# A recurrence on four quarters of the matmul array, with block-diagonal operands for two heads at once

## The reference, cut to what matters

```python
def step(state, inp):
    r_t, w_t, k_t, v_t, kk_t, a_t = inp
    sa = jnp.einsum('bhvk,bhk->bhv', state, -kk_t)
    state = (state * w_t[:, :, None, :]
             + sa[..., None] * (kk_t * a_t)[:, :, None, :]
             + v_t[..., None] * k_t[:, :, None, :])
    return state, jnp.einsum('bhvk,bhk->bhv', state, r_t)
_, y = lax.scan(step, s0, tuple(map(seq_first, (r, decay, k, v, kk, a))))
```

## Time and profile before

| what | value |
|---|---|
| median of 3 runs | 2769.58 us |
| the profiled execution's own time | 2771.98 us |
| its span (first to last record) | 2770.1 us |
| PE busy | 2617.0 us (94%), 28073 records |
| PEld busy | 2190.7 us (79%) |
| VectorE, ScalarE, GpSimd busy | 1563.2, 1318.0, 316.2 us |
| `rwkv` | from about 1210 to about 1762 us of the span |

### The profile page before, as it was taken

The page is one execution under the profiler, slowest core; times in us unless marked ns, Lnnn a source line. Parts: engine busy times, 40 slices in busy tenths (PEclk is TensorE's granted clock), DMA queues, the critical chain, the costliest instruction groups (busy, mean ns, idle before and its releaser), DMA issues. The chain is left out here.

```text
span 2770.1 us, 66149 instructions
## 1 busy us (share of the span) xinstructions
PE 2617.0 (94%) x28073; PEld 2190.7 (79%) x28073; DVE 1563.2 (56%) x2377; ACT 1318.0 (48%) x2272; POOL 316.2 (11%) x367
## 2 busy tenths in 40 slices
PE   6999999999999999989999999999999999999992
PEld 5989897777766766678999998888888888888882
DVE  4566664443035555544444444553326888888884
ACT  4645552222134444334444444552223777777771
POOL 0111222332000000001212121100001000000002
PEclk9999999999999999999999999999998999999996
DMA  4344332222132323313221201154345999999976
GB/s 111 148 167 145 125 138 89 92 93 74 37 96 65 99 68 102 114 38 81 55 69 52 64 21 33 48 152 129 121 185 219 397 395 395 395 396 395 395 301 258
DMA packets 162649, 440.53 MB, mean 159 GB/s; under 512 B 16295, under 2 KB 96825, under 8 KB 150097
## 3 DMA queue, kind: packets, MB, share of 16 engines
q1 hardware_dynamic: 146413, 381.95, 38.7%
q10 hardware_dynamic: 9060, 29.56, 2.8%
q0 software_dynamic: 6912, 25.17, 2.4%
HBM read 344.22 MB, written 92.41 MB: 158 GB/s over the span
## 5 line engine op out<-in xcount | busy, mean ns | idle before, releaser
L2671 DVE TENSOR_TENSOR ex_wL<-wx,ex_wH 128x2048 fp32r<-128x2048 f32 x192 | 436.1, 2286 | 46.5 <-ACT ex_wH L2575 43.8
L2575 ACT CAST ex_wH<-wx 128x2048 fp32r<-128x2048 f32 x192 | 366.4, 1912 | 96.3 <-PE ex_bank L2467 70.7
L2465 PE MATMUL ex_bank<-ex_wH,ex_xTH 128*128 128x512 f32 x512 | 199.4, 389 | 0.6 <-DVE ex_xTL L2676 0.6
L2467 PE MATMUL ex_bank<-ex_wL,ex_xTH 128*128 128x512 f32 x512 | 199.3, 389 | 0.0
L2466 PE MATMUL ex_bank<-ex_wH,ex_xTL 128*128 128x512 f32 x512 | 199.2, 389 | 0.0
L717 PE MATMUL ph_acc<-ph_wH,uH 128*104 128x512 f32 x480 | 191.5, 399 | 0.0
L717 PE MATMUL ph_acc<-ph_wH,uL 128*104 128x512 f32 x480 | 188.8, 393 | 0.0
L717 PE MATMUL ph_acc<-ph_wL,uH 128*104 128x512 f32 x480 | 188.6, 393 | 0.0
L419 PE MATMUL pf_acc<-uH,pf_wH 128*128 128x348 f32 x648 | 160.7, 356 | 6.4 <-DVE pf_wL L541 6.4
L419 PE MATMUL pf_acc<-uL,pf_wH 128*128 128x348 f32 x648 | 138.9, 323 | 0.0
L419 PE MATMUL pf_acc<-uH,pf_wL 128*128 128x348 f32 x648 | 138.3, 322 | 0.0
(11 more groups left out here) (416 smaller groups left out, 6879.5 us busy)
## 6 DMA issues: line engine op xcount, KB each, us to landing
wx<-in_expert_w_gate SPq DMA_DIRECT2D x32, 2048.0 KB
wx<-in_expert_w_up SPq DMA_DIRECT2D x32, 2048.0 KB
wx<-in_expert_w_down SPq DMA_DIRECT2D x32, 2048.0 KB
s_y<-ex_y ACTq DMA_DIRECT2D x32, 512.0 KB, 10.0
fw<-in_w_in SPq DMA_DIRECT2D x27, 512.0 KB
hw<-in_w_in SPq DMA_DIRECT2D x6, 2048.0 KB, 10.1
s_qkT<-ph_stg ACTq DMA_DIRECT2D x4, 2080.0 KB, 7.0
mb_gt<-s_pT SPq DMA_DIRECT2D x16, 512.0 KB, 3.6
```

The source lines that it names most:

```text
L2465: nc.tensor.matmul(out, aH, bH, start=first, stop=False)
L2467: return nc.tensor.matmul(out, aH, bL, start=False, stop=last)
L2575: nc.scalar.copy(wH[:, w, part], raw(j, s)[:, part]).then_inc(w_high, 1)
L2671: nc.vector.tensor_tensor(wL[:, w, part], raw(j, s)[:, part], wH[:, w, part], ALU.subtract).then_inc(w_low, 1)
```

## The change

- Inputs: one set of buffers instead of two. The next four heads' inputs are loaded in five pieces of 4 chunks (10 DMAs each), each piece when `seq` has passed its chunks. `x_in` becomes five semaphores.
- Place of a head: `across(e, h)` says on which half of the partitions the token-side data of head h of pair e lie: h for e = 0, 1 - h for e = 1. So products from channels to tokens (or back) of the four heads use all four quarters of the array: `masked`, the new `raw` (the old step 2), piece 1 of `seq`, the state update, the new `old_state`. The two pairs write different banks (0 and 1, or 6 and 7).
- Block-diagonal operands: `Md`, `Nd`, `Yd`, `Gd` hold the two heads' matrices on the diagonal of a 116 x 116 matrix whose rest is zero, so that one product over the full array serves both heads: steps 9, 11, 12, the masked products of `seq`, and piece 3. They are written in two instructions, one for each half of the partitions.
- `tokens`: GpSimd copies each input twice side by side (`two`, 3 copies a chunk), and six full-array transposes replace twelve small products. ScalarE takes the result out in two copies.
- Step 7 makes one product with 104 columns out of two (`X2` now has `Q0`'s matrix in its middle).
- `seq` has four pieces. The masked product with v of piece 1 is made one chunk ahead, in piece 2. R is made on VectorE, the old state's part of Y is a product of its own (`old_state`), copied by ScalarE (`Hs`) and added on VectorE. The new state and Y are in piece 4 together.
- A round has 8 pieces among its groups. Bank 7's role for `tokens` and the norm's transposes passes to banks 0 and 1, shared by `masked`, `raw`, `tokens`, `old_state` and the norm: each waits until the one before it has been read (`after_reading`).
- GpSimd clears `two`, `tok`, most of `Md`, `Nd`, `Yd` and `Gd` at the start of `rwkv` (8960 elements for each partition).
- In `project_recurrent` the norm's two parameter rows are loaded with 32 DMAs instead of 8, in the new order of heads; `load_branch` follows that order.

The diff, cut to its core:

```diff
+                    for e, h in ((0, 0), (0, 1), (1, 0), (1, 1)):
+                        at = NF * j + 2 * d + across(e, h)
+                        sp.dma_start(rows_[at:at + 1, RD * e:RD * e + RD], heads[e, h:h + 1]).then_inc(consts, 16)
...
+def across(e, h):
+    return h if e == 0 else 1 - h
...
-            return (first(2) + late(9) + tokens(A) + piece()
-                    + first(6) + late(10) + ahead(A + 2, 0) + piece()
-                    + first(7) + late(11) + ahead(A + 2, 1) + piece()
-                    + first(8) + late(12) + piece() + piece()
...
+            return (tokens(A) + copies(A + 2) + first(6) + late(10) + piece() + old_state(A - 2)
+                    + first(7) + raw(B) + late(11) + piece()
+                    + first(8) + late(12) + piece()
+                    + ahead(A + 2) + first(9) + piece()
+                    + tokens(B) + copies(B + 2) + second(6) + first(10) + piece() + old_state(B - 2)
+                    + second(7) + raw(A + 2) + first(11) + piece()
+                    + second(8) + first(12) + piece()
+                    + ahead(B + 2) + second(9) + piece())
...
+            def masked(ch):
...
+                for j in range(2):
+                    for e, h in PAIRS:
+                        last = mm(bank[row(e, h), e, 2 * j * TC:(2 * j + 2) * TC].rearrange("p (a t) -> p a t", a=2),
+                                  BK[half(h), e, j, cols], KR[half(h), e, :, cols], start=True, stop=True)
...
+            def raw(ch):
+                after_reading(n_read, ch + 1 + OPEN)
+                for e, h in PAIRS:
+                    last = mm(bank[row(e, h), e, 0:TC], KR[half(h), e, 0, cols], BK[half(h), e, 0, cols], start=True, stop=True)
...
-                    for e, h in PAIRS:
-                        last = mm(at(bq, 0, e, h), N8[here(h), ln, e, :], Q[here(h), ln, 0, e, :], start=True, stop=True)
+                    for e in range(2):
+                        last = mm(full(bq, e), both(Nd[0:PX, ln, e]), Q[0:PX, ln, 0, e, :], start=True, stop=True)
...
+            def tokens(ch):
+                after_reading(tok_read, ch + 1 + OPEN)
+                pe.wait_ge(twice, 3 * ch + 4 + OPEN)
+                for e in range(2):
+                    for j in range(3):
+                        last = tr(bank[0:PX, e, RD * (1 - e) + 2 * RD * j:RD * (1 - e) + 2 * RD * (j + 1)], two[:, ch % 3, e, j].rearrange("p n t -> p (n t)")[:, 0:PX], c.ident[:])
...
+            def seq(ch, q):
+                if q == 1:
...
+                        pe.wait_ge(y_done, ch + OPEN)
+                        pe.wait_ge(seq_dve, added(ch - 1))
+                        for e, h in PAIRS:
+                            last = mm(bank[row(e, h), 6 + e, 384:384 + RD], KR[half(h), e, 0, cols], S[half(h), t % 2, e, :], start=True, stop=True)
+                elif q == 2:
+                    pe.wait_ge(rest_done, ch + 1 + OPEN)
                     for e, h in PAIRS:
+                        last = mm(o(1, e)[here(across(e, h))], Qf[row(e, h), s, e, :], R[row(e, h), e, :], start=True, stop=True)
+                    if ch + 1 < NC:
+                        for e in range(2):
+                            last = mm(o(2, e), both(Md[0:PX, (ch + 1) % MS, e, 1]), tok[0:PX, (ch + 1) % TS4, 2, e, :], start=True, stop=True)
                 elif q == 3:
+                    for e in range(2):
+                        last = mm(o(0, e), both(Gd[0:PX, s, e]), RA[0:PX, 0, e, :], start=True, stop=True)
                 else:
+                    if t < NCH - 1:
+                        for j, right in ((0, lambda e, h: Uu[row(e, h), e, :]), (1, lambda e, h: tok[row(e, h), s, 2, e, :])):
+                            for e, h in PAIRS:
+                                mm(bank[half(h), 6 + e, 128:128 + RD], tok[row(e, h), s, j, e, :], right(e, h), start=(j == 0), stop=(j == 1))
                     for e in range(2):
+                        mm(o(2, e), both(Md[0:PX, m, e, 2]), tok[0:PX, s, 2, e, :], start=True, stop=False)
+                        last = mm(o(2, e), both(Md[0:PX, m, e, 0]), Uu[0:PX, e, :], start=False, stop=True)
...
+            def old_state(ch):
+                after_reading(h_read, carried(ch))
+                for e, h in PAIRS:
+                    last = mm(bank[row(e, h), e, 0:RD], KR[half(h), e, 1, cols], S[half(h), ch % NCH % 2, e, :], start=True, stop=True)
...
+            nc.gpsimd.memset(two[:], 0.0).then_inc(twice, 1)
+            nc.gpsimd.memset(tok[:], 0.0).then_inc(blank, 1)
+            nc.gpsimd.memset(Md[:, 2:MS], 0.0).then_inc(blank, 1)
+            nc.gpsimd.memset(Nd[:], 0.0)
+            nc.gpsimd.memset(Yd[:], 0.0).then_inc(blank, 1)
+            nc.gpsimd.memset(Gd[:], 0.0).then_inc(blank, 1)
```

More of the change, by code:

```diff
@@ L1306, in round_ @@
             A, B = 2 * r, 2 * r + 1
-            pieces = iter([(2 * r - 2 + j, q) for j in range(2) for q in (1, 2, 3, 4, 5)])
+            pieces = iter([(2 * r - 2 + j, q) for j in range(2) for q in (1, 2, 3, 4)])
             first = lambda n: [("solve", A, n)] if new else []
@@ L1323, in rwkv @@
-        SPREAD = {"sum0": 0, "sum1": 1, "mean": 2, "sub": 2, "sq": 3, "var0": 8, "var1": 9, "std": 11, "rin": 12, "nrm": 12,
-                  "t0": 17, "e0": 17, "t1": 18, "e1": 18, "t2": 24, "e2": 24, "add": 25, "gate": 25}
+            old_state = lambda ch: [("h", ch)] if old and ch % NCH > 0 else []
+            copies = lambda ch: [("two", ch)] if new and ch < NC else []
+            return (tokens(A) + copies(A + 2) + first(6) + late(10) + piece() + old_state(A - 2)
[6 more added lines that the diff above has]
+                    + ahead(B + 2) + second(9) + piece())
@@ L1465, in solve @@
-                last.then_inc(spe[ln], 1)
-            last_read = [(tok_emptied, 1 + OPEN)]
-            def tokens(ch):
-                d, z, cols = place(ch)
-                for x in last_read:
-                    pe.wait_ge(*x)
-                for j in range(3):
-                    for e, h in PAIRS:
-                        src = V[z][half(h), e, cols] if j == 2 else BK[z][half(h), e, j, cols]
-                        last = mm(bank[here(h), 7, (2 * j + e) * RD:(2 * j + e + 1) * RD], src, c.ident[half(h), half(h)], start=True, stop=True)
-                last.then_inc(tok_done, 1)
-                last_read[:] = [(tok_read, ch + 1 + OPEN)]
@@ L1548, in solve @@
                 four = bank[0:PX, bx, 0:4 * TC].rearrange("p (k e t) -> p k e t", k=2, e=2)
-                two = bank[0:PX, bx, 0:2 * TC].rearrange("p (e t) -> p e t", e=2)
-                what = {6: (X2[0:PX, ln], four), 7: (X4[0:PX, ln], four), 8: (N8[0:PX, ln], two),
-                        10: (Y1[0:PX, ln], two)}
+                two = bank[:, bx, 0:2 * TC].rearrange("p (e t) -> p e t", e=2)
+                what = {6: (X2[0:PX, ch % TS4, 0::2], four), 7: (X4[0:PX, ln], four)}
+                if n in (8, 10):
+                    act.wait_ge(*at_pe(ch, n))
+                    if ch < 2:
+                        act.wait_ge(blank, 4 + OPEN)
+                    for h in range(2):
+                        last = nc.scalar.copy((Nd if n == 8 else Yd)[here(h), ln, :, h, 0:TC], two[here(h)])
+                    last.then_inc(sact[ln], 1)
                 if n in what:
@@ L1653, in norm, with copies @@
                 ins.then_inc(gn["pool"], 1)
-            walk({"m": masked, "gn": norm})
+            def copies(ch):
+                d, cols = place(ch)
+                if d > 0 and ch % PIECE == 0:
+                    pool.wait_ge(x_in[ch % NCH // PIECE], 160 * d + OPEN)
+                if ch >= 3:
+                    pool.wait_ge(tok_done, ch - 2 + OPEN)
+                for e in range(2):
+                    nc.gpsimd.tensor_copy(two[:, ch % 3, e, 0:2, :, 0:TC], BK[:, e, :, cols].unsqueeze(2).to_broadcast([128, 2, 2, TC])).then_inc(twice, 1)
+                nc.gpsimd.tensor_copy(two[:, ch % 3, :, 2, :, 0:TC], V[:, :, cols].unsqueeze(2).to_broadcast([128, 2, 2, TC])).then_inc(twice, 1)
+            nc.gpsimd.memset(two[:], 0.0).then_inc(twice, 1)
[4 more added lines that the diff above has]
+            nc.gpsimd.memset(Gd[:], 0.0).then_inc(blank, 1)
+            pool.wait_ge(twice, 1 + OPEN)
+            walk({"two": copies, "m": masked, "gn": norm})
         @block.vector
```

347 lines of the change are left out of this document (185 added, 162 removed).

## The result

The changed kernel takes 3080.5 us (median of 3069.0 to 3116.2), the kernel before 2769.8: a ratio of 1.111, 95% interval 1.1086 to 1.1135. The forecast was 2922 us, the range 2790 to 2990. The direction was right; the time is 159 us above the forecast and outside the range.

What follows compares the result with a forecast made beforehand. PE was taken to bound `rwkv`, 95 to 96% busy at full clock. Chunks going from 6.76 to 8.6 us add 145 us, the start 8: 2771.98 becomes 2925, less 2.4 for the median, 2922 us; range 2790 to 2990.

Steps and rivals of the forecast that it cites:

- the period: Time from chunk to chunk in `rwkv`: 8.6 us instead of 6.76, from PE's work, norm transposes, waits and issue.
- Records of block-diagonal products, 0.10 us each: Weight load sets the pace of 28 full-array records a chunk: 2.80 us, where the same work took 1.50.
- (b): Rival: weight load of the block-diagonal records is hidden, 1.50 us a chunk instead of 2.80; 2820 us, chance 0.10.
- (c): Rival: full-array products cost only moving columns, tiling changes fall into gaps, copies and adds set the pace; 2717 us, chance 0.14.
- Changes of tiling, 0.145 us each, 10 a chunk: PE pays at each switch between quarter and full-array products: 1.45 us a chunk.
- Four quarters, twice as fast: `masked`, `raw`, piece 1, state update and `old_state` on all four quarters: 0.92 us a chunk instead of 1.83.
- rival (a): Third and fourth quarter bring nothing, no record starts sooner than 24 ns: 33 us more, 2955 us, chance 0.12.
- Waits 0.6 us, on `Hs` before `raw`: PE waits for ScalarE's copy to free the bank: 0.6 us a chunk in all, 0.1 of it before step 7.
- Start, 8 us: Once, at the start of `rwkv`: GpSimd's clearing and copies delay the first `tokens`, PE idles; 8 us, bounds 0 and 12.
- SyncE's added DMAs, 0: 24 more parameter-row DMAs of 0.29 us, ahead of the third tile's weights, nearly fit: 0 us, at most 3.
- Tokens 0.65: Six full-array token transposes in `tokens`: 0.65 us a chunk, against 0.69 before.
- VectorE and ScalarE still waiting for PE: Sign in `rwkv`: VectorE rising to 4.6 us a chunk and ScalarE to 4.4, both below PE's.

Runs made afterwards that it cites:

- run 1: Changed kernel with steps 9, 11 and 12 as two-quarter products out of the same block-diagonal buffers; 2899.7 us.
- run 14: Changed kernel with all block-diagonal products as two-quarter ones in the first 20 of 80 chunks, unchanged from chunk 20 on; 3011.0 us.
- run 6: Changed kernel with the products of steps 6, 8 and 10 issued twice, 24 more two-quarter products a chunk; 3108.7 us.
- run 11: run 8 with its 12 added full-array products a chunk moving 4 columns each in place of 52; 3371.9 us.
- run 9: Changed kernel with one pair of neighbouring products in `seq` swapped, 8 changes of tiling a chunk in place of 10; 3062.7 us.
- run 10: run 9 with step 9 also issued ahead of the masked products, 6 changes of tiling a chunk, all products kept; 3016.6 us.
- run 2: run 1 with the state's and the output's products as two-quarter products too; 2843.3 us.
- run 7: run 4 with 12 more full-array products of 52 columns a chunk, all ahead of step 9, results unread; 2904.3 us.
- run 8: run 7 with the same 12 added products in six pairs at six places, 12 changes of tiling where run 7 has 2; 3074.8 us.
- run 3: run 2 with the token transposes as twelve four-quarter products, one ScalarE copy instead of two, no GpSimd copies; 2807.8 us.
- run 4: run 3 with compact buffers in place of block-diagonal ones, fewer mask and copy instructions, no clearing of the buffers; 2773.2 us.
- run 13: run 8 with the 12 added full-array products only from chunk 20 of 80 on; 2915.5 us.
- run 12: run 4 with the next layer pair's inputs loaded in two pieces of 10 chunks in place of five of 4; 2782.7 us.

## Why the prediction was wrong

**The step that failed is the period.** "Period: 7.75 + 0.09 + 0.6 + 0.15 = 8.6 us" took every duration from rows at the full clock and multiplied by 79 as if the clock were given. The forecast names no clock at all. The changed stage holds the lower level for 41% of its time, and that is 128 of the 161 us by which the profiled execution missed (3086.2 against 2925). That the block-diagonal products bring it there is shown: with three steps of them undone the clock is back (run 1), and switched on from chunk 20 they bring it down again (run 14). Runs 6 and 11 show one thing that matters: with 48 fewer streamed columns a product the low level holds longer, and with more streamed products less of it is left. PE is 94 to 96% busy in all of these, so the busy share, on which the forecast leaned, can't tell.

What sets off each single fall is not shown. In the changed kernel and in runs 1, 6, 9, 10 and 14, every fall inside the stage comes within 4 us behind a wait for `Hs` of at least 0.5 us, or in one. The wait alone isn't enough (run 1, 73 waits and 2 falls; run 2, 92 and 1), and run 11 fell without. So few streamed (moving) columns beside many weight loads, and a wait on top, is the account that fits all the runs; it is argued and not shown. No run here takes the wait for `Hs` out of the changed kernel; that is the rival left untested.

Point by point:

- *Records of block-diagonal products, 0.10 us each*: right. 0.103 in run 7, 0.11 in the changed kernel. (b) and (c) are refuted.
- *Changes of tiling, 0.145 us each, 10 a chunk*: the count is right, the price too high. 0.08 us by runs 7 and 8, about 0.10 by L1473.
- *Four quarters, twice as fast*: right for 104 columns (0.022 us a record against 0.045). For the 52 columns of `raw` it is 0.022 against 0.024, nearly what rival (a) said. For 64 columns four records take 0.097 us in `old_state` and 0.082 on the mean in the state update, against 0.115. The Trainium skill, "TensorE: Matmul & The Clock Gate", section "Wait — 56ns, not 53.3ns?", has about 25 ns as the least distance from start to start. Taken singly, starts in different quarters lie 7 ns apart here, so the trace disagrees; taken over whole bursts, the four quarters need 20 to 24 ns a record.
- *Waits 0.6 us, on `Hs` before `raw`*: the place is right, 0.4 us measured there.
- *The sum at the full clock, 8.6*: 8.96 measured, within the 7.5 to 9.5 that was given; 29 us over the stage. The trace says where, if each record is given the time to the next one's start (us a chunk, the 32 chunks at 1.00, changes of tiling at 0.145 in the forecast):

```
                                        forecast                measured
four quarters, 3 changes behind them    0.92 + 0.44 = 1.36      1.69
two quarters, 2 changes                 1.93 + 0.29 = 2.22      2.41
block-diagonal, 4 changes               2.80 + 0.58 = 3.38      3.41
tokens, 1 change                        0.65 + 0.15 = 0.80      0.76
norm transposes                         0.09                    0.10
waits and issue                         0.60 + 0.15 = 0.75      0.59
```

  The largest mis-sized term is the four quarters: the new piece 1 and `old_state`, forecast at 0.115 us each, take 0.29 and 0.30 to the next start. Behind piece 1 the next weight load often waits for ScalarE's token copy while PE still counts as busy (PEld for `rw_tok`, 46 times in the stage, 10.4 us in all); the rest of the cause is open.
- *Start, 8 us*: 10, but 5.6 in the stage itself. *SyncE's added DMAs, 0*: what they cost is lost in the 4.5 us that arose before the stage, within the 6 us by which that point varies.
- *Tokens 0.65*: L1498 to L1448 is 0.75, a change included.
- *"VectorE and ScalarE still waiting for PE"*: right in the changed kernel, but their doubled instructions would have been the next bound: 35 us (runs 3 to 4), the start's share included.
- *What was not foreseen at all*: the range, 2790 to 2990, allowed each price to be wrong but not the rate at which all of them are paid.

The Trainium skill, "TensorE: Matmul & The Clock Gate", section "HAM oscillation — how this bites in real kernels", ties a clock that falls again and again to idle gaps between bursts of products. PE's waits here are short: the longest in the changed stage is 2.2 us and most are 0.5 to 0.7, and in run 11 it is busy 260.00 of 260.00 us at 0.50. So idle gaps of that size aren't what holds the clock down; that the falls come behind short waits fits a part for them. The measurement decides against reading that rule as the only cause.

## What to carry to other kernels

Before merging small products into wide ones, count the columns that each weight load serves, and the places where the tiling changes: 52 columns behind 116 weight columns cost 0.10 us where two small ones side by side cost 0.05, and each place 0.08 more. Where a change puts weight loads and changes of tiling in place of streamed columns, forecast it at both levels of the clock: here a chunk is 8.96 us at one and 14.2 at the other, and the granted clock, not the busy share, tells which it is. Put full-array products next to each other (58 us of the loss came back by order alone), and keep the good part by itself: in four quarters the 16 masked records take 0.51 us to the next start (1657.95 to 1658.46), a change of tiling included, where they took 0.72. With 52 columns four quarters gain little (`raw`).

## What the chip showed unexpectedly

- More work made the kernel hardly longer: 24 more products a chunk, +34 us (run 6). Less streaming made it much longer: 48 columns fewer in 12 products a chunk, +297 us (run 11).
- The clock's level can hold itself. The load of run 8 stood at 1.2 GHz for 280 us and at 2.4 GHz for 550 us after it, and at 2.4 GHz throughout when entered so (run 13). What ends such a stretch was not found.
- In the changed kernel every fall of the clock inside the stage comes in or right behind a wait of half a microsecond or more, yet most such waits bring none.
- Records for the four quarters start in bursts of four, 7 ns apart, and a burst costs 86 to 89 ns to the next one whether it moves 52 or 104 columns (L1430, L1422). The 24 ns of the earlier trace rows is a mean over pairs, not a least distance.
- TensorE with 27433 records where the kernel before has 28073, and less time for many of them, stands idle more often with nothing named as the cause (22 us before, 58 in run 4), whatever the length of the DMA packets beside it (68 in run 12).
